# Output projection and feed-forward with channels on the partitions, the second norm's inverse behind the gate and up products

## The reference, cut to what matters

```python
def merge_and_ffn(x, conv_out, attn_out, w_out, ffn_norm_g, w_gate, w_up, w_down):
    mix = jnp.concatenate([conv_out, attn_out.astype(conv_out.dtype)], axis=-1)
    x = x + jnp.einsum('bte,ed->btd', mix, w_out)
    h = rms_norm(x, ffn_norm_g)
    f = jax.nn.silu(jnp.einsum('btd,df->btf', h, w_gate)) * jnp.einsum('btd,df->btf', h, w_up)
    return x + jnp.einsum('btf,fd->btd', f, w_down)
```

## Time and profile before

| | |
|---|---|
| median of three executions | 1814.24 us |
| profiled execution | 1811.3 us |
| its span (first to last instruction) | 1809.5 us |
| mean granted TensorE clock | 0.936 |
| TensorE matmuls busy | 1611.4 us, 89% |
| VectorE / ScalarE / GpSimd busy | 48% / 24% / 23% |
| output projection | 866.1 to about 966.3 us |
| feed-forward | 994.0 to 1809.5 us |

### The profile page before, as it was taken

One profiled execution on the slowest core, in us unless ns is written; L12 is line 12 of the kernel. 1 busy time (PEld: TensorE's weight loads), 2 busy tenths in 40 slices (PEclk: granted clock), 3 DMA queues, 4 the chain that ended last, 5 costly groups with the idle time before them and its releaser, 6 DMA issues.

```text
span 1809.5 us, 22777 instructions
## 1 busy us (share of the span) xinstructions
PE 1611.4 (89%) x8473; PEld 1386.0 (77%) x8473; DVE 861.8 (48%) x1452; ACT 431.1 (24%) x792; POOL 416.8 (23%) x273
## 2 busy tenths in 40 slices
PE   4999988879957788666996999999999999999999
PEld 3998767447757677632675989989899899898997
DVE  5299889998679965400126033231331322313223
ACT  4100268554265435511013101001010010010100
POOL 5332111401410000021016222323223232132210
PEclk9999999889968778877997999999999999999999
DMA  6212101200220010066302111101111111111102
GB/s 198 77 37 72 51 15 28 76 12 24 91 111 13 6 51 1 5 191 203 110 24 70 35 35 46 46 23 58 46 35 46 44 48 36 35 58 35 46 0 99
DMA packets 112689, 101.17 MB, mean 56 GB/s; under 512 B 12041, under 2 KB 96329, under 8 KB 112487
## 3 DMA queue, kind: packets, MB, share of 16 engines
q1 hardware_dynamic: 104314, 92.26, 16.6%
q10 hardware_dynamic: 8309, 8.08, 1.4%
HBM read 87.65 MB, written 13.02 MB: 56 GB/s over the span
## 4 chain that ended last, share of the span: by engine, by line
PE 50%; DVE 4%; issue 2%; ACT 1%; SPq 1%; DMA 0%; DVEq 0%; ACTq 0%
PE ps L797 16%; PE ps L799 16%; PE ps L798 16%; PE ps L1190 1%; PE ps L1148 1%; DVE f_lo L2128 1%; DVE x L2135 1%; DVE xn L1605 1%; DVE lo_t L1615 1%; SPq L494 0%; SPq L619 0%; DMA kt_b<-in_cache_kt 0%; PE ps L1174 0%; DVE lo_t L2038 0%; ACT sq L1253 0%
## 5 line engine op out<-in xcount | busy, mean ns | idle before, releaser
L797 PE MATMUL ps<-hi_t,w_hi 128*128 128x384 f32 (+3 forms) x1272 | 417.0, 328 | 5.9 <-ACTq L1574 3.4
L799 PE MATMUL ps<-hi_t,w_lo 128*128 128x384 f32 (+3 forms) x1272 | 416.8, 328 | 0.0
L798 PE MATMUL ps<-lo_t,w_hi 128*128 128x384 f32 (+3 forms) x1272 | 416.7, 328 | 0.0
L2144 DVE TENSOR_TENSOR ff<-ps,sg 128x384 f32<-128x384 f32 (+1 forms) x66 | 35.4, 536 | 466.6 <-PE ps L799 466.6
L797 PEld LDWEIGHTS ps<-hi_t,w_hi 128*128 128x128 f32 (+1 forms) x1272 | 239.3, 188 | 8.3 <-ACTq L1574 3.8
L798 PEld LDWEIGHTS ps<-lo_t,w_hi 128*128 128x128 f32 (+1 forms) x1272 | 239.3, 188 | 1.1
L799 PEld LDWEIGHTS ps<-hi_t,w_lo 128*128 128x128 f32 (+1 forms) x1272 | 239.2, 188 | 0.6
L2135 DVE TENSOR_TENSOR x<-x,ps 128x512 f32<-128x512 f32 (+1 forms) x198 | 134.9, 685 | 123.3 <-PE ps L799 123.3
L782 POOL CAST w_hi<-w_raw 128x1024 fp32r<-128x1024 f32 x60 | 62.3, 1039 | 537.2 <-PE ps L799 537.2
L797 PE MATMUL ps<-w_hi,hi_t 128*128 128x512 f32 (+1 forms) x400 | 158.4, 396 | 13.3 <-DVEq L1775 5.3
L797 PE MATMUL ps<-w_hi,f_hi 128*128 128x512 f32 (+1 forms) x396 | 157.6, 398 | 6.8 <-DVE x L2135 6.8
(11 more groups left out here) (270 smaller groups left out, 2318.2 us busy)
## 6 DMA issues: line engine op xcount, KB each, us to landing
w_raw<-in_w_in SPq DMA_DIRECT2D x24, 512.0 KB, 3.6
w_raw<-in_w_gate SPq DMA_DIRECT2D x22, 512.0 KB, 3.8
w_raw<-in_w_up SPq DMA_DIRECT2D x22, 512.0 KB, 3.8
w_raw<-in_w_down SPq DMA_DIRECT2D x22, 512.0 KB, 3.5
kt_b<-in_cache_kt SPq DMA_DIRECT2D x64, 128.0 KB, 2.4
v_b<-in_cache_v SPq DMA_DIRECT2D x40, 128.0 KB, 3.8
xin<-in_x_prompt SPq DMA_DIRECT2D x8, 512.0 KB, 4.2
w_raw<-in_w_out SPq DMA_DIRECT2D x8, 512.0 KB, 5.0
```

Of the source, the lines that this page charges most:

```text
L797: pe.matmul(out, a_hi, b_hi, start=first, stop=False)
L798: pe.matmul(out, a_hi, b_lo, start=False, stop=False)
L799: return pe.matmul(out, a_lo, b_hi, start=False, stop=last)
L2144: dve.tensor_tensor(ff[:, m % 2, 0:z - a], ps[:, 3 + m % 3, 0:z - a], sg[:, m % 2, 0:z - a], ALU.mult).then_inc(f_ready, 1)
```

## The change

1. **Projection.** The weight becomes stationary and hi_t, lo_t stream. A unit of w_out is now all 1024 input channels by 128 output channels (512-byte runs). Steps s = 0 to 23 go over output channel block m and BLOCKS j, in bank s mod 8. x1 lies with channels on the partitions; x_t, a transposed copy of x laid out by the host, is loaded for it in 8 transfers.
2. **Sum of squares.** ScalarE squares each step's piece of x1, VectorE adds the pieces in ssq. TensorE adds over the partitions with nine matmuls of one column (`row_sums`), placed behind the first gate block. VectorE and GpSimd make the inverse, VectorE diagonals of it, TensorE spreads them over the partitions (`row_scales`, placed behind the third gate block, three tiles at a time), ScalarE copies them to rs_all.
3. **Split.** hi_t and lo_t of x1 * g, without the inverse, by ScalarE (8 pieces a block) and VectorE (`split_rows`). No transposes.
4. **Gate and up.** VectorE multiplies gate by rs_all into sg (`scale_gate`), ScalarE takes silu in place, VectorE multiplies by rs_all again (`scale_silu`), so that the up product is scaled too, and then with up. sg has three places instead of two. Group 0 is written out, groups 1 to 10 are a loop.
5. **Down.** w_down is stationary, f streams. 24 steps q of six matmuls: BLOCKS j outside, channel block m inside, banks 6 and 7 in turn. 24 additions to x1 instead of 18.
6. **Output.** y is stored with channels first, blocks 0 and 1 whole, block 2 in 8 pieces. The host transposes it.

The core of the diff:

```diff
-            project(5, N_OUT, 512, x1_ready)
-            project(6, N_OUT + 4, 512, x1_ready)
-            pe.wait_ge(x1_ready, 2 * NT)
-            for o in range(NT):
-                transpose_rows(NT + o, xn1[0:rows_of(ALL[o]), o % NX1, :], rows_of(ALL[o]))
-            pe.wait_ge(hi_ready, 2 * NT)
-            pe.wait_ge(lo_ready, 2 * NT)
+            for s in range(NDOWN):
+                m, j = divmod(s, NB)
+                a, z = BLOCKS[j]
+                if j == 0:
+                    pe.wait_ge(split_lo, N_OUT + m + 1)
+                if s >= 8:
+                    pe.wait_ge(x1_added, s - 7)
+                for k in range(KT):
+                    mm = three(ps[:, s % 8, 0:z - a], *unit(N_OUT + m, k, P), hi_t[:, k, a:z], lo_t[:, k, a:z],
+                               k == 0, k == KT - 1)
+                mm.then_inc(out_mm, 1)
+            def row_sums():
+                pe.wait_ge(ssq_added, NDOWN)
+                pe.wait_ge(x1_added, NDOWN)
+                for t in range(NT):
+                    r = rows_of(t)
+                    mm = pe.matmul(ps[0:r, 4, t:t + 1], ssq[:, cols_of(t)], ones[:, 0:1], start=True, stop=True)
+                mm.then_inc(var_mm, 1)
+            def row_scales():
+                for t in range(NT):
+                    a = BLOCKS[t // 3][0]
+                    r = rows_of(t)
+                    if t % 3 == 0:
+                        pe.wait_ge(lnd_ready, NB + t // 3 + 1)
+                    mm = pe.matmul(ps[:, (6, 7, 5)[t // 3], t * P - a:t * P - a + r], ones[0:r, :], diag1[0:r, t % 3, 0:r],
+                                   start=True, stop=True)
+                    if t % 3 == 2:
+                        mm.then_inc(lnb_mm, 1)
+                    if opening and 2 * c + gu == 0:
+                        pe.wait_ge(lo_ready, NT + KT * (j + 1))
+                    if opening and (c, gu, j) == (0, 1, 2):
+                        pe.wait_ge(rs_ready, NT + NB)
...
-                for t in range(NT):
-                    r = rows_of(t)
-                    for nh in range(2):
-                        pe.wait_ge(y_added, g * (2 * NT) + (1 + max(0, 2 * t + nh - 1)))
-                        for c in range(2):
-                            n = N_FFN + 4 + c
-                            mm = three(ps[0:r, 6 + nh, :], f_hi[:, c, cols_of(t)], f_lo[:, c, cols_of(t)],
-                                       *unit(n, nh, 512), c == 0, c == 1)
+                for j, (a, z) in enumerate(BLOCKS):
+                    pe.wait_ge(f_hi_ready, g * 6 + (4 + j))
+                    pe.wait_ge(f_lo_ready, g * 6 + (4 + j))
+                    for m in range(KT):
+                        q = KT * j + m
+                        pe.wait_ge(y_added, g * NDOWN + (1 + max(0, q - 1)))
                         for c in range(2):
+                            mm = three(ps[:, 6 + q % 2, 0:z - a], *unit(N_FFN + 4 + c, m, P), f_hi[:, c, a:z], f_lo[:, c, a:z],
+                                       c == 0, c == 1)
                         mm.then_inc(down_mm, 1)
...
+            def split_rows(j):
+                a, z = BLOCKS[j]
+                for k in range(KT):
+                    dve.wait_ge(hi_ready, NT + KT * j + k + 1)
+                    dve.scalar_tensor_tensor(lo_t[:, k, a:z], x1[:, k, a:z], kf[:, K_GF + k:K_GF + k + 1],
+                                             hi_t[:, k, a:z].bitcast(F32), ALU.mult, ALU.subtract).then_inc(lo_ready, 1)
...
+            for s in range(NDOWN):
+                m, j = divmod(s, NB)
+                a, z = BLOCKS[j]
+                if j == 0 and m % 4 == 0:
+                    dve.wait_ge(x_in[m // 4], 16 * (3 + 4))
+                dve.wait_ge(out_mm, s + 1)
+                dve.tensor_tensor(x1[:, m, a:z], x1[:, m, a:z], ps[:, s % 8, 0:z - a], ALU.add).then_inc(x1_added, 1)
+                if s > 0:
+                    add_ssq(s - 1)
+                if m == KT - 1 and j > 0:
+                    split_rows(j - 1)
+            add_ssq(NDOWN - 1)
+            split_rows(NB - 1)
...
+                for c in range(2):
+                    for m in range(3 * c, 3 * c + 3):
+                        scale_gate(m)
+                        if m > 3 * c:
+                            scale_silu(m - 1)
+                        if m == 4:
+                            take_f_lo(2)
+                    scale_silu(3 * c + 2)
+                    for m in range(3 * c, 3 * c + 3):
+                        multiply(m)
+                        if m > 3 * c:
+                            take_f_lo(m - 1)
+                dve.wait_ge(y_added, g * NDOWN + 1)
+                add_down(0)
+                add_down(1)
                 take_f_lo(5)
+                for q in range(2, NDOWN):
+                    add_down(q)
```

More of the change, by code:

```diff
@@ L71 @@
 SEL = [SAMPLE] + list(range(FIRST, S // P))
-CHUNKS = [[], SEL, SEL, ALL, ALL, ALL, ALL]
-NX1 = 7
-BASE = [sum(len(c) for c in CHUNKS[:i]) for i in range(8)]
+CHUNKS = [[], SEL, SEL, ALL, ALL]
+BASE = [sum(len(c) for c in CHUNKS[:i]) for i in range(6)]
+NB = len(BLOCKS)
+NDOWN = NB * KT
 COUNT_ACT = (2, 4)
@@ L436, in decoder_program @@
         mixs_lo = sem("mixs_lo")
-        x1_ready = sem("x1_ready")
+        out_mm = sem("out_mm")
+        x1_added = sem("x1_added")
+        sq1_ready = sem("sq1_ready")
+        ssq_added = sem("ssq_added")
+        gate_taken = sem("gate_taken")
+        sg_ready = sem("sg_ready")
         gate_mm = sem("gate_mm")
@@ L685, in used @@
                     return u_mm, 3 * (n - N_U + 1)
-                c, i = divmod(n - N_QI, 4) if n < N_OUT else divmod(n - N_OUT, 4)
-                late = 0 if n < N_OUT else 4
-                return (w_used, 3 * (c + late) + i + 1) if i < 3 else (proj_done, BASE[c + late + 2])
+                if n >= N_OUT:
+                    return out_mm, NB * (n - N_OUT + 1)
+                c, i = divmod(n - N_QI, 4)
+                return (w_used, 3 * c + i + 1) if i < 3 else (proj_done, BASE[c + 2])
             def split(n):
@@ new lines, in gate_up @@
+            def gate_up(g, opening, c, gu):
+                n = N_FFN + 2 * c + gu
+                pe.wait_ge(split_lo, g * 6 + (n + 1))
+                for j, (a, z) in enumerate(BLOCKS):
+                    done = 3 * c + j
+                    pe.wait_ge(f_ready if gu else gate_taken, g * 6 + (1 + max(0, done - 2)))
+                    if opening and 2 * c + gu == 0:
[3 more added lines that the diff above has]
+                    for k in range(KT):
+                        mm = three(ps[:, 3 * gu + j, 0:z - a], *unit(n, k, P), hi_t[:, k, a:z], lo_t[:, k, a:z],
+                                   k == 0, k == KT - 1)
+                    mm.then_inc(up_mm if gu else gate_mm, 1)
+                    if opening and (c, gu, j) == (0, 0, 0):
+                        row_sums()
+                    if opening and (c, gu, j) == (0, 0, 2):
+                        row_scales()
@@ L1210, in _, with ffn_group @@
+            def ffn_group(g, opening):
                 for c in range(2):
                     for gu in range(2):
-                        n = N_FFN + 2 * c + gu
-                        pe.wait_ge(split_lo, g * 6 + (n + 1))
-                        for j, (a, z) in enumerate(BLOCKS):
-                            done = 3 * c + j
-                            pe.wait_ge(f_ready if gu else silu_f, g * 6 + (1 + max(0, done - 2)))
-                            for k in range(KT):
-                                w = unit(n, k, P)
-                                mm = three(ps[:, 3 * gu + j, 0:z - a], *w, hi_t[:, k, a:z], lo_t[:, k, a:z],
-                                           k == 0, k == KT - 1)
-                            mm.then_inc(up_mm if gu else gate_mm, 1)
@@ L1237, in _ @@
                         mm.then_inc(down_mm, 1)
+            pe.sem_inc(down_mm, 1)
+            ffn_group(0, True)
+            with pe.Fori(1, FG) as g:
+                ffn_group(g, False)
         @block.scalar
@@ L2116, in _, with add_ssq @@
-            for o in range(NT):
-                if 5 <= o + 3 < NT:
-                    norm_x1(o + 3)
-                take_lo(NT + o)
+            def add_ssq(s):
+                m, j = divmod(s, NB)
+                a, z = BLOCKS[j]
+                dve.wait_ge(sq1_ready, s + 1)
+                if m == 0:
+                    dve.sem_inc(ssq_added, 1)
+                else:
+                    dve.wait_ge(ssq_added, s - NB + 1)
+                    dve.tensor_tensor(ssq[:, a:z], ssq[:, a:z], sq1[:, s % 2, 0:z - a], ALU.add).then_inc(ssq_added, 1)
```

234 lines of the change are left out of this document (122 added, 112 removed).

## The result

| | before | after |
|---|---|---|
| median (four executions each) | 1814.62 us | 1796.47 us |
| range | 1814.18 to 1816.35 | 1796.04 to 1799.51 |
| profiled execution | 1811.3 us | 1799.51 us |
| its span | 1809.5 us | 1797.7 us |

The ratio is 0.9902 [0.9885, 0.9919]: 18 us faster, 1.0%. The forecast was 1776 us, with 1793 as its upper end. About half of the expected gain is there. The profiled execution of before is not one of its four timed ones.

A forecast was written before the change was run, and what follows sets the result against it. TensorE was taken to bound the end, through matmul count and start-to-start time, the hole, and small down-product stops. Terms -3.3 - 19.3 - 15.4 = -38.0 gave 1776 us for the median, range 1765 to 1793.

The forecast's parts named there:

- w_out's runs: w_out loads between the cache loads on SP's queue: shorter runs priced at 0, bound -1 to +2 us.
- the hole: TensorE's idle stretch between output projection and feed-forward: from 30.3 to 11 us, -19.3, bounds 7 and 20.
- The projection: Output projection with the weight stationary: 97.9 us before, 94.6 after, -3.3 us.
- the tail: Kernel's end, with a shorter last addition and a smaller last store: 0, bound -1 to +2 us.
- VectorE's turnaround: Down products: about 0.8 us fits within each step; as a rival, at 1.6 it paces them, 1846 us, chance 0.06.
- The second scaling: Gate and up: VectorE's added work, 6 us per group, lies under other work and costs 0.
- Row sums: In the hole, after the first gate block: 2.1 us idle before the sums, which take 1.8 us.
- the first stop: TensorE waits for split_rows(0) between projection and first gate matmul: 1.9 us idle.
- a rival of 20 us: Hole filled poorly: GpSimd holds two-input VectorE operations and the clock falls again; hole 20 us, total 1785, chance 0.12.
- The down products: Feed-forward's down products with w_down stationary: 24.7 us per group against 26.1, 11 x -1.4 = -15.4 us.
- The new stops: TensorE's stops at the start of each group's down products: 1.1 us with restarts, bounds 0.4 and 2.1.
- form cost stays: Rival in the down products: the old form's 20 ns per matmul remain, +11 us, 1787 us, chance 0.17.

The follow-up runs named there:

- the last one: Changed kernel with long w_out runs, two GpSimd splits and last f_lo later, nine diagonal places, earlier split_rows, later row_sums and row_scales: 1763.34 us, ratio 0.9726.

## Why the prediction was wrong, by its own steps

The forecast was 1776 us in a range up to 1793, and 1796.47 was measured. Two of its terms were mis-sized, w_out's runs and the hole, and a third thing, the spread of the upstream stretch, had no term.

**What held.** The projection (-3.3 forecast, -3.1 measured) and the tail (from the last matmul to the end 4.0 us, before 4.5). VectorE's turnaround paced nothing. The second scaling cost nothing. Row sums came without a wait, where I had feared 2.1 us. With GpSimd out of the way the first stop is 1.93 us, my 1.9, and the hole 10.5 against my 11; the latter is partly luck, since it has no wait ahead of the row sums and 3.3 us at half clock instead.

**w_out's runs, the first step that failed.** "I price that at 0, bound -1 to +2" was 6.8. I compared how long such a unit takes to land on an idle queue (3.8 us for w_gate), not what stands behind it. SP issues keys, w_out and values in one order, and the last keys end a wait of TensorE's. One of the rounds grew by 2.4 us, the last keys' way to TensorE by 2.1, and 2.0 followed at a lower clock; with long runs all three are gone. The landing of w_gate was the wrong row; the one to read was the w_out issue beside the key loads on SP's queue, with the question what a longer issue moves. The upper bound of +2 had no row behind it.

**The hole, the second.** I named the right mechanism and gave it, with the clock falling again, a rival of 20 us and a chance of 0.12; 19.6 is what came. The step that failed is where the block falls. I set split_rows(0) at 4 us, done at T + 1.9, and GpSimd's split at T to T + 3.5. These overlap by 1.9 us by my own figures: the last three or four of the eight run beside the split. Yet I charged the block to split_rows(1) only. The measured order was just this: T at 980.8, GpSimd from 981.11, split_rows(0) held until 985.6. I didn't lay the next split against row_scales at all, and set its diagonals at 0.28 each. And I left out the clock: the earlier trace rows showed half clock behind the old hole, which I counted there (2.7 us) and not in the new one, where 15 matmuls at 0.32 instead of 0.173 lost 2.2 us and row_scales' stop about as much again.

The Trainium skill (SBUF — State Buffer, "Who interferes with whom") says that a VectorE instruction with two SBUF inputs contends with a GpSimd instruction that reads SBUF, and that such contention is an exclusive lock. The trace agrees: the longest of the eight took 2.69 us against GpSimd's 2.53 and its own 0.6. The diagonals have only one full tile among their inputs, beside a column, so that sentence doesn't speak of them; but the third of the second set took 2.36 us instead of 0.28 and ended 0.08 us behind the split.

**The down products: right total, two wrong terms.** I had 24.7 us per group, the rows give 24.80. But the form's own time was forecast at 23.6 and is 24.33: a step of 384 columns takes 1.06 us, 0.1767 per matmul and not 0.173 (one of 320 columns takes 0.88, as forecast), and 0.3 us more are not in the steps' pitch. The new stops were forecast at 1.1 and are 0.47 (24.80 - 24.33). That the total came out is luck: the errors cancel. The form's part, old and new without stops, is 25.19 - 24.33 = 0.86 us per group where I had 1.6, about 9.5 us in 11; the rest of the gain, 0.95 less 0.47, came from the order of VectorE's instructions; a swap in the old kernel brings 0.95 by itself. The rival "form cost stays" (1 us per group) was thus true for 0.7 of it.

**The base.** I took the spread of this kernel as 0.2%, from three executions. Over 45 later ones the kernel before ran from 1802.8 to 1817.5 us, 0.8%. The first pair of profiles set a long upstream stretch of after beside a usual one of before. Taking the upstream stretch out of both leaves -22.8 us for the change (-22.5 with the repeated profile), against -18 and -19 between the medians. These 4 us stay open: no experiment shows an upstream cost of the change, and none excludes one of 2 to 4 us.

**The sum again, with measured terms:** +6.8 for w_out, -3.1, -11.6, -14.7: -22.6. With the 7.1 us that w_out's layout gives back and the 9.5 of the moved splits it is -39, about the forecast, and the version with both measured 1769.37 beside 1811.22 of before: -42, with an interval of 4 us either way.

## What to carry to other kernels

A shorter run length was paid in good part on the queue that issues it, so ask which loads stand behind it and which of them an engine waits for. Before costing a chain at its unblocked durations, write the other engine's instructions that read SBUF on the same time line and shift whichever overlaps; here a move of two splits was worth as much as the new matmul form. Look at a stop's neighbours in program order first: swapping two instructions of the old kernel took 0.6% (10 us), and one more such move in the new one took 5 us.

## What the runs showed of the hardware that I had not expected

- A matmul with 384 moving columns behind its own weight load starts 0.1767 us after the one before in the down products and 0.173 in the gate blocks; with 320 columns it is 0.147 in both, and with 512 it was 0.2333 in the old down products and 0.2267 in the old projection.
- Two issues of 512 KB on SP's queue took 1.08, 2.83 and 1.52 us with 512-byte runs, and 0.93 to 0.98 with longer ones, and landed in 7.5 instead of 5.5 to 5.7 us.
- The stops of 4.8 and 3.2 us and both of 1.93 were followed by a stretch at half clock (1.2 of 2.4 GHz); those of 0.77 and 0.73 in the version with moved splits and of 0.18 in the last one weren't. In one version 2 us of one-column matmuls were followed by such a stretch too, in the others not.
- The kernel before spreads over 0.8% in 45 executions. The granted clock in the same 200 us of three kernels' profiles was 0.89 to 0.93, the lowest in the one that was latest behind it; that the clock makes the spread is likely and not shown.
